# Order of the leftover strips in the expert steps of a decoder trunk: after the main down products instead of before them

## The reference, cut to what matters

```python
combine = sum(one_hot(expert_id) * weights)                # (N, 16), two nonzero entries in a row
for wg, wu, wd, c in experts:                              # lax.scan over 16 experts
    y = (silu(x @ wg) * (x @ wu)) @ wd
    acc = acc + c[:, None] * y
x = x + acc
y_out = x * rsqrt(mean(x * x) + EPS) * final_g
```

## Time and profile before

| what | value |
|---|---|
| median of 3 runs | 942.31 us (940.86 to 948.8) |
| the profiled execution | 942.12 us, its span 940.4 us |
| TensorE matmul busy | 867.6 us (92% of the span) |
| TensorE weight load busy | 714.2 us (76%) |
| VectorE busy | 533.4 us (57%) |
| ScalarE busy | 371.2 us (39%) |
| GpSimd busy | 237.3 us (25%) |
| HBM traffic | 147.39 MB read, 41.17 MB written |

### The profile page before, as it was taken

The page is one execution under the profiler, slowest core; times in us unless marked ns, Lnnn a source line. Parts: engine busy times, 40 slices in busy tenths (PEclk is TensorE's granted clock), DMA queues, the critical chain, the costliest instruction groups (busy, mean ns, idle before and its releaser), DMA issues. The chain is left out here.

```text
span 940.4 us, 15242 instructions
## 1 busy us (share of the span) xinstructions
PE 867.6 (92%) x5544; PEld 714.2 (76%) x5544; DVE 533.4 (57%) x1235; ACT 371.2 (39%) x692; POOL 237.3 (25%) x269
## 2 busy tenths in 40 slices
PE   4997999999999979999739999999999999999992
PEld 3567785666676658788539999999999989999992
DVE  5336743454775473554467566766665656666551
ACT  5446422344435242344312444333344434324441
POOL 1000000000000010000013464546445645455461
PEclk9998999999999979999859999999999999999996
DMA  8510105011000056093316888899888978989850
GB/s 266 157 46 1 45 0 135 1 45 45 1 24 23 1 168 239 1 313 135 113 56 220 315 297 297 284 351 326 290 282 285 325 262 302 329 294 313 290 207 23
DMA packets 118694, 167.07 MB, mean 178 GB/s; under 512 B 14996, under 2 KB 98040, under 8 KB 118661
## 3 DMA queue, kind: packets, MB, share of 16 engines
q1 hardware_dynamic: 103301, 136.03, 42.9%
q0 software_dynamic: 15360, 30.59, 9.4%
HBM read 147.39 MB, written 41.17 MB: 201 GB/s over the span
## 5 line engine op out<-in xcount | busy, mean ns | idle before, releaser
L1694 PE MATMUL bank<-big,ring 128*128 128x160 f32 x2048 | 285.8, 300 | 1.7 <-DVE x L1977 1.3
L1694 PEld LDWEIGHTS bank<-big,ring 128*128 128x128 f32 x2048 | 281.3, 191 | 3.4 <-DVE x L1977 1.4
L461 PE MATMUL bank<-big,ring 128*128 128x384 f32 (+1 forms) x480 | 152.9, 473 | 0.0
L461 PEld LDWEIGHTS bank<-big,ring 128*128 128x128 f32 x480 | 90.7, 192 | 53.8 <-issue 4.6
L1619 POOL TENSOR_TENSOR hold_at<-ident 128x1 f32<-128x1 f32 x63 | 56.5, 897 | 179.8 <-DVE lists L1845 119.7
L1907 DVE TENSOR_TENSOR wdlo<-wdn,split 128x1024 fp32r<-128x1024 f32 x64 | 76.6, 1218 | 0.0
L1792 ACT CAST split<-wdn 128x1024 fp32r<-128x1024 f32 x64 | 64.9, 1040 | 0.0
L1273 PE MATMUL bank<-split,ahi 128*128 128x512 f32 (+1 forms) x144 | 58.7, 408 | 4.4 <-DVE split L1391 4.4
L1788 ACT ACTIVATE sg<-bank 128x160 f32<-128x160 f32 x64 | 19.5, 304 | 102.4 <-PE bank L1694 102.2
L1274 PE MATMUL bank<-split,ahi 128*128 128x512 f32 (+1 forms) x144 | 57.9, 402 | 0.0
L1275 PE MATMUL bank<-split,alo 128*128 128x512 f32 (+1 forms) x144 | 57.7, 401 | 0.0
(11 more groups left out here) (333 smaller groups left out, 1526.9 us busy)
## 6 DMA issues: line engine op xcount, KB each, us to landing
wdn<-in_w_down SPq DMA_DIRECT2D x32, 1024.0 KB, 9.5
ring<-in_w_gate SPq DMA_DIRECT2D x32, 1024.0 KB, 6.0
ring<-in_w_up SPq DMA_DIRECT2D x32, 1024.0 KB, 10.6
x<-in_x_prompt SPq DMA_DIRECT2D x16, 512.0 KB, 7.0
ring<-in_w_in SPq DMA_DIRECT2D x8, 1024.0 KB, 8.7
ring<-in_w_out SPq DMA_DIRECT2D x4, 1024.0 KB, 5.0
h_rows<-h SPq DMA_DIRECT2D x8, 512.0 KB, 2.6
sums<-x SPq DMA_DIRECT2D x8, 512.0 KB, 3.6
```

The lines of the kernel that those rows point to most:

```text
L461: mm = nc.tensor.matmul(acc(n)[:, 0:tn], ring[:, u % 4, k, c0:c0 + P], hT[:, k, t0:t0 + tn], start=k == 0, stop=k == KC - 1)
L1694: x = nc.tensor.matmul(bank[f % 2][:, side * 256:side * 256 + W], ring[:, u, k, c0:c0 + P], xT[:, k, :], start=k == 0, stop=k == KC - 1)
```

## The change

Three queues get another order. On TensorE the wait for the last `hid` and `left_down` move from before the 24 main `down` matmuls to behind them. On VectorE the addition of `z2` moves behind the two additions of `z`. On ScalarE the Square of `z2` moves behind the Square of both halves of `z` and behind the first Sqrt. The counts in the waits for `e_z` follow. Nothing is added or taken away, and SyncE and GpSimd keep their code; but SyncE's wait for `e_yl` is now met later in the order of TensorE.

```diff
@@ tensor, step @@
-            pe.wait_ge(e_h, i * 4 + 5)
-            left_down()
             for h in range(2):
                 for k in range(4):
                     if h == 0:
                         pe.wait_ge(e_wl, i * 4 + k + 1)
                         pe.wait_ge(e_hl, i * 4 + k + 1)
                     down(h, k)
+            pe.wait_ge(e_h, i * 4 + 5)
+            left_down()
@@ scalar @@
-            act.wait_ge(e_z, i * 3 + 2)
-            nc.scalar.activation(squares2[:], z2[:], ACT.Square, scale=D ** -0.5,
-                                 accum_out=ssq[:, 2:3]).then_inc(e_sql, 1)
             for h in range(2):
-                act.wait_ge(e_z, i * 3 + h + 3)
+                act.wait_ge(e_z, i * 3 + h + 2)
                 nc.scalar.activation(squares[:, h * 512:(h + 1) * 512], z[:, h * 512:(h + 1) * 512], ACT.Square,
                                      scale=D ** -0.5, accum_out=ssq[:, h:h + 1]).then_inc(e_sq, 1)
             act.wait_ge(e_s0, i + 1)
             act.wait_ge(e_sq, i * 2 + 2)
             nc.scalar.activation(root[:, 0:1], ssq[:, 1:2], ACT.Sqrt, bias=ssq[:, 3:4]).then_inc(e_rt, 1)
+            act.wait_ge(e_z, i * 3 + 4)
+            nc.scalar.activation(squares2[:], z2[:], ACT.Square, scale=D ** -0.5,
+                                 accum_out=ssq[:, 2:3]).then_inc(e_sql, 1)
             act.wait_ge(e_ms, i + 1)
             nc.scalar.activation(root[:, 1:2], bank[6][:, 2 * P:2 * P + 1], ACT.Sqrt, bias=eps_c[:]).then_inc(e_rt, 1)
@@ vector, step @@
-            dve.wait_ge(e_yl, i + 1)
-            nc.vector.scalar_tensor_tensor(out=z2[:], in0=bank[1][:, 0:CW], scalar=weight_now[:, 1:2], in1=old2[:],
-                                           op0=ALU.mult, op1=ALU.add).then_inc(e_z, 1)
             for h in range(2):
                 dve.wait_ge(e_y, i * 2 + h + 1)
                 nc.vector.scalar_tensor_tensor(out=z[:, h * 512:(h + 1) * 512], in0=bank[2 + h][:, :],
...
                 if h == 0:
                     dve.wait_ge(e_sq, i * 2 + 1)
                     nc.vector.tensor_tensor(ssq[:, 3:4], ssq[:, 0:1], eps_c[:], ALU.add).then_inc(e_s0, 1)
+            dve.wait_ge(e_yl, i + 1)
+            nc.vector.scalar_tensor_tensor(out=z2[:], in0=bank[1][:, 0:CW], scalar=weight_now[:, 1:2], in1=old2[:],
+                                           op0=ALU.mult, op1=ALU.add).then_inc(e_z, 1)
```

## The result

The changed kernel takes 973.41 us in the median (971.09 to 985.64, 4 runs) where the kernel before takes 944.38 (940.86 to 948.8, 4 runs): a ratio of 1.033, with a 95% interval of 1.023 to 1.043. It is slower by 3.3%; the forecast was 948.3, with a range of 940 to 958.

What follows compares the result with a forecast made beforehand. TensorE's own order was taken to bound the kernel. Terms 7.0 (`e_sql` wait) + 0.7 (lost slack) + 1.5 (GpSimd) - 3.0 (last step) = +6.2 us on 942.12 gave 948.3 us, range 940 to 958.

Steps and rivals of the forecast that it cites:

- GpSimd's term: Late `wdn` delays the sums' landing and so `e_free`, for which VectorE waits: 1.5 us taken, plus 0.7 for lost slack.
- rival A: GpSimd's chain becomes the pace, late `wdn` delaying the sums' landing about 0.8 us in most steps: 957 us, chance 0.27.
- The `e_sql` wait: TensorE waits at `left_sums` for ScalarE's Square until 5.2 us after S (VectorE's additions start): 0.5 us a step, 7.0 total.
- Rival B: The wait at `left_sums` hardly bites; only the tail's gain and some lateness remain: 940 us, chance 0.15.
- The tables: On ScalarE, a Square between two Sqrts reloads no activation tables; costed at nothing.
- rival C: ScalarE's tables are reloaded, Square and second Sqrt each adding 1.28 us: 967 us, chance 0.03.
- The tile form changes: Idle gaps on TensorE where tile form changes: costed at nothing, bounds a gain of 0.57 and a loss of 0.41 us a step.
- The last step: Main products no longer wait for the last `hid` and `left_down`, so the last scaling comes 3.0 us earlier.
- ScalarE and wdn: `wdn` is issued about 5.4 us later but lands in time for ScalarE; nothing directly on TensorE.

Runs made afterwards that it cites:

- the results first: Changed kernel, but GpSimd sends its results before it waits for the sums' landing and gathers the next sums: 946.47 us; same edit in the kernel before: 942.45 us.
- half the delay: Kernel before, but SyncE waits for the first half of the main down product before loading `wdn`: 946.39 us, ratio 1.003.
- early `wdn`: Changed kernel, but `left_down` reads the weights' high parts (`wdhi`) and SyncE no longer waits for `e_yl` before loading `wdn`: 947.79 us, ratio 1.002.
- `wdn` behind the sums: Changed kernel, but SyncE also waits for the landing of the sums before it loads `wdn`: 983.18 us, ratio 1.042.
- the kernel with the early Square: Changed kernel, but ScalarE squares `z2` ahead of the first Sqrt and its table load: 989.16 us, ratio 1.045.
- the one with late `wdn` alone: Kernel before, but SyncE waits for the second half of the main down product before loading `wdn`; no engine's order changed: 973.41 us, ratio 1.032.

## Why the prediction was wrong

**The step that failed is GpSimd's term, taken at 1.5 us with bounds of nothing and 11.** The changed kernel and the same with the results first differ by 973.4 less 946.5, 27 us. Some 2 us of that the kernel before pays as well (944.4 less 942.5 with its results first), so about 25 us stand against the sum's 0.7 and 1.5 for GpSimd, more than twice the upper bound. The forecast put most chance on its staying small; rival A had the mechanism and its place right (chance 0.27), but with 957 us it too was short of the measured time. A's even lateness, 0.8 us in most steps, is not what the trace shows either: the cost fell on a few steps.

Three things made it so far off.

1. *The landing.* I read from the earlier trace rows only how long GpSimd waited, not what the two queues did in those microseconds. Before, loads and indirect transfers did not share the engines: the loads had them until S + 4 and GpSimd's packets after. The late `wdn` made them share from S + 4 to S + 10 or 11. Of that sharing the Trainium skill, page "DMA: Bandwidth & Descriptors", section "Queues, rings and completion order", says that an engine goes in turn through the queues that have work. The shares of 51% and 41% from S + 4 to S + 11 agree. From S to S + 4 only loads ran, though the gathers were issued from S + 0.1 on; whether these had work in the queue by then the trace does not show. What I drew from it, that the sums would be late only by the `wdn` packets left behind them, missed that the gather of rows stands ahead of the sums in the same queue and is slowed as well. GpSimd's wait for the sums rose by 24.9 us in 15 steps, 1.7 a step where I had allowed 0.8 at most.
2. *The threshold.* I counted the 10 steps without a wait for `e_free` as room. In the kernel before, an undisturbed step has `lists_now` at S + 21.2 to 21.3, and in steps 6, 10 and 13 the results had landed only 0.4 to 0.6 us ahead of it. In steps 7, 8 and 11 results sent last at S + 16.6 already made it 22.3 to 24.4; in steps 1, 4 and 12, sent as late, they did not. So the landing of the results varies too: of those sent at S + 16.6 to 16.8 the last took 2.5 to 7.5 us. In the changed kernel VectorE waited for `e_free` in 7 steps, 19.0 us, where it had waited in 6, 7.7 us. The waits became long rather than many: the three longest, 15.1 us in all, stand in the three steps whose results were sent last, at S + 19.4, 20.7 and 23.4, and so behind SyncE's issue of the next `ring` loads at S + 18.9. Whether these loads slow the landing of the results was not tried. That half the delay costs 2 us and the whole 28 shows the corner.
3. *The clock.* In its step 1 TensorE went idle at 549.7 and waited to 557.2. In that wait the granted clock fell to 0.50 (1.2 GHz), and it came back only some 4 us after the work had begun again. The windows of the kernel after, of 2 us each, show it (the clock is the third number from the end):

```profile
553.00:555.00 2.00, 0.00 (x0) 0.00 (x0) 1.21 (x3) 1.11 (x4) 1.18 (x3) 0.76 0.55 106
555.00:557.00 2.00, 0.00 (x0) 0.00 (x0) 0.13 (x1) 1.97 (x6) 1.16 (x3) 0.50 0.57 221
557.00:559.00 2.00, 1.78 (x7) 1.78 (x8) 1.88 (x4) 1.28 (x4) 0.95 (x1) 0.50 0.42 158
559.00:561.00 2.00, 2.00 (x10) 2.00 (x9) 0.41 (x2) 1.87 (x4) 1.39 (x3) 0.54 0.00 0
561.00:563.00 2.00, 2.00 (x17) 2.00 (x16) 1.42 (x2) 0.00 (x0) 1.82 (x3) 1.00 0.77 233
```

From `left_sums` to `indices` it took 15.0 us there and 16.1 in step 10, where an undisturbed step takes 13.24: 1.8 and 2.9 us beyond the waits themselves. Behind S of step 14 it happens a third time (15.94 in place of 13.07 us for f = 1 to 3). I had costed waits at their own length. That the clock fell because TensorE stood idle is read from the order of the rows in these traces; no run tries it by itself.

**The `e_sql` wait** was right to 0.03 us: `left_sums` at S + 5.17 against S + 5.2 by the sum, and 27.3 us a step wherever GpSimd was in time (the kernels with TensorE's order put back, with early `wdn`, and with the results first). Rival B falls.

**The tables** were not reloaded: one load for Sqrt in each step and one for Silu in each but the last; rival C falls.

**The tile form changes** were costed at nothing. Of two kernels with the early Square and the results first, the one with `left_down` in its old place has 26.83 us a step, the one with the late order 26.76; the gain of 0.07 a step was within my bounds.

**The last step** was right: 3.0 us by the sum, 3.00 by the rows. The wait and the slower clock behind S of step 14 outweighed it.

**ScalarE and wdn.** The prediction has `e_yl` near S + 0.6; its own numbers, S - 5.1 and 5.4 later, give S + 0.3, and undelayed steps had `wdn` issued at S + 0.35. In the changed kernel ScalarE waited once for the weights, 2.8 us; the cover I had named was there. The run with `wdn` behind the sums shows where it ends: issued at S + 7 in place of S + 0.4, the loads are waited for 30 times.

**What stays open.** How 32 us divide between the landing, the waits and the clock was not tried run by run. By the lengths of the intervals in the trace, the 28 us above 27.33 a step are some 21 in the seven intervals in which VectorE waited for `e_free`, 4.8 in the two behind the long waits, where the clock was lower, and 2 elsewhere; the other 4 are the longer undisturbed steps (7 us) less the lateness that the kernel before had (3.1). In step 5 of the changed kernel ScalarE's fourth Silu and SyncE's loads came some 1.6 us later than TensorE's records let one expect; I have no explanation. Why the kernel with the early Square and the one with late `wdn` alone fell into the pattern of two steps, and the changed kernel only three times, was seen and not tried.

## What to carry to other kernels

A product moved behind another one also moves the release of the buffer that it reads, and with it a transfer: look up what else is on the DMA engines at the new time before costing the move at nothing. A chain with a transfer in it that ends about half a microsecond ahead of its need, as in steps 6, 10 and 13 of the kernel before, is not room but an edge. Sending the results without waiting for another transfer to land took away all waits for `e_free` here, and only with that order was a kernel with the moved product faster than the kernel before, by 0.3%. And a row "TensorE waited for ScalarE" names the last link, not the cause: the Square was the releaser in the changed kernel, and mending it alone made the kernel 16 us slower.

## What the runs showed of the hardware that I had not expected

The gathers' first packets came late only beside loads. In the step of the changed kernel that begins at 665.05 the gathers were issued from S + 0.1 and `wdn` at S + 0.35; the loads' packets begin near S + 1.3, and q0 has none before S + 4, though the engines were nearly idle at first. In the same kernel's step that begins at 552.05, with hardly any loads running, q0 has its first 14 packets between S + 1 and S + 2. What holds the gathers back beside the loads no run shows.

And a wait of TensorE at `left_sums` cost more than its length when it was long. Three in the changed kernel (4.75, 6.20 and 7.54 us) and seven in the kernel with the early Square (4.0 to 6.2 us) were each followed by some 3 to 6 us of work at the granted clock of 0.50 (1.2 GHz), which made the stretch behind them 1.6 to 3.2 us longer. The waits of 1 to 2 us, of which the changed kernel has five, left the clock at 1.00 (2.4 GHz) in the same trace.
